# Convolution FFNs: high weights times high and low h as one 512-column matmul, sum kept in SBUF

## The chip, the cores and the metric

The kernel runs on one core of one Trainium2 chip. The metric is the device time of one execution in microseconds. A profile of one execution gives the start and duration of each instruction on TensorE (PE, with its weight loads as PEld), VectorE (DVE), ScalarE (ACT) and GpSimd (POOL), and the DMAs.

## The reference, cut to what matters

Two blocks of two layers each work on 256 positions of width 1024 in float32. Each layer of the first block ends with a feed-forward network whose up product goes through a causal depthwise convolution of three taps, before the gate:

```
h = _rmsnorm(x, norm_ffn[l]) * (1 + sc_f) + sh_f
u = _causal_dwconv(h @ ffn_w_up[l], ffn_conv_w[l], ffn_conv_b[l])   # 3 taps over time, plus a bias
ua, uv = jnp.split(u, 2, axis=-1)
x = x + g_f * ((jax.nn.silu(ua) * uv) @ ffn_w_down[l])
```

`h @ ffn_w_up` is 256 x 1024 by 1024 x 5632, the down product 256 x 2816 by 2816 x 1024. Each layer of the second block has two feed-forward networks of the same sizes without the convolution: `(silu(x @ w1) * (x @ w3)) @ w2`. So there are two convolution FFNs and four plain ones, and one piece of code, `ffn`, serves both kinds (`conv` true or false).

## The kernel before, in words

Everything is held transposed, features on the 128 partitions and the 256 positions (T) in the free dimension. An FFN is cut into 22 units (NJ = 22). Unit j takes 128 columns of the first half of the up weights (half 0, which goes through silu), 128 of the second half (half 1), and 128 rows of the down weights: 24 tiles of 128x128, one slot of 1.5 MB in a ring of four slots which SyncE fills.

A float32 product is made from three float32r products: weights and activations are split in a high and a low part, and high x high, high x low and low x high are summed. For each unit:

- ACT copies the up weights (L660, 2048 columns) and the down weights (L673, 1024 columns) to the high tile `w_hi`; DVE subtracts to get `w_lo` (L711, L716). Both tiles have two places, j % 2.
- PE's `up_pair` makes the up product of both halves. Where `conv` holds it goes by `narrow_half` (L597): for each half 8 matmuls w_hi x h_hi, 8 w_hi x h_lo, 8 w_lo x h_hi, all of 256 columns into the same 256 columns of PSUM, both halves in one bank (4 + j % 2). Plain FFNs go by `wide_half`: `hh` holds h_hi and h_lo side by side, and 8 matmuls of 512 columns (L606) give both products side by side in a bank of their own; 8 of 256 columns (L610) add w_lo x h_hi to the first 256. Only half 0 of the first unit is narrow there.
- Plain: ACT copies columns 256 to 511 to `cv` in SBUF (L685), DVE adds columns 0 to 255 to it (L742). ACT's silu (L688), DVE's product (L746).
- Convolution: ACT reads the product in PSUM, times the last tap plus the bias, into `cv` (L679, scale and bias are columns of `par`). DVE adds the other two taps, reading PSUM shifted by one and by two positions (L729, L734; two instructions each, one for each half). ACT's silu (L682), DVE's product (L746).
- Both: ACT makes `g_hi` (L693), DVE `g_lo` (L751), and PE's `down` multiplies (L634, 24 matmuls of 256 columns into banks 0 to 3, which accumulate over the 22 units).

The order is written out by hand and each engine works in order. PE: up of unit j + 1, then down of unit j. ACT for unit j: up weights of unit j + 1, down weights of j, `cv`, silu, `g_hi`. DVE for unit j: `w_lo` up of unit j + 1, `w_lo` down of j, the taps or adds, product, `g_lo`. Units 0, 1 and 18 to 21 are written out ("peeled"); units 2 to 17 run on ACT and DVE in a hardware loop of four units a turn, where the columns of `par` are addressed through registers. After unit 21 DVE adds the result to `x` (L849), which ends the stage; the next stage needs all of `x`.

Of the kernel before, what the change touches and what calls it, by code (L numbers as in the profile page):

```python
# [18 lines left out]
ALU = mybir.AluOpType  # L19
ACT = mybir.ActivationFunctionType  # L20
AX = mybir.AxisListType.X

P = 128
T = 256
# [193 lines left out]
def build(nc, A, out, layers1=LAYERS, layers2=LAYERS, dump=None):  # L218
    ctx = ExitStack()
    with ctx:  # L220
# [51 lines left out]
        def S(name):  # L272
            if name not in sems:
                sems[name] = scope[-1].enter_context(nc.semaphore(name))
            return sems[name]
# [301 lines left out]
        UP = slice(0, 2 * UNIT)  # L577
        DOWN = slice(2 * UNIT, 3 * UNIT)

        def up_out(j, half, conv):  # L580

            return bank[4 + j % 2][:, half * T:half * T + T] if conv else bank[4 + 2 * (j % 2) + half][:, :]

        def ffn_pe(pe, tag, conv):

            def narrow_half(j, half, free, first):

                for n, (w_, part) in enumerate(((w_hi, 0), (w_hi, 1), (w_lo, 0))):
                    if n == 2:
                        pe.wait_ge(*free)  # L590
                    for k in range(KD):
                        if first and n < 2:
                            pe.wait_ge(*(h_lo_ready(tag, k) if part else (S(tag + "_h_hi"), k + 1)))
                        c0 = half * UNIT + k * P
                        out = up_out(j, half, conv)
                        cols = slice(0, T) if conv or part == 0 else slice(T, 2 * T)
                        m = pe.matmul(out[:, cols], w_[:, j % 2, c0:c0 + P], hh[:, k, part, :],  # L597
                                      start=n == 0 and k == 0, stop=n == 2 and k == KD - 1, skip_group_check=True)
                return m

            def wide_half(j, half, free):

                out = up_out(j, half, conv)
                for k in range(KD):
                    c0 = half * UNIT + k * P
                    pe.matmul(out, w_hi[:, j % 2, c0:c0 + P], hh[:, k, :, :], start=k == 0, stop=False)  # L606
                pe.wait_ge(*free)
                for k in range(KD):
                    c0 = half * UNIT + k * P
                    m = pe.matmul(out[:, 0:T], w_lo[:, j % 2, c0:c0 + P], hh[:, k, 0, :], start=False,  # L610
                                  stop=k == KD - 1)
                return m

            def up_pair(j, lo_n, free_n=None, first=False):
                pe.wait_ge(S(tag + "_up_hi"), lo_n)
                if free_n is not None:
                    pe.wait_ge(S(tag + "_whole"), free_n)
                for half in range(2):
                    if first and half == 1:
                        pe.wait_ge(S(tag + "_first_hi"), 1)  # L620
                    low = (S(tag + "_first_lo"), 1) if first and half else (S(tag + "_up_lo"), lo_n)
                    if conv or (first and half == 0):
                        m = narrow_half(j, half, low, first and half == 0)
                    else:
                        m = wide_half(j, half, low)
                m.then_inc(S(tag + "_up"), 1)

            def down(j, n, first=False, last=False):
                pe.wait_ge(S(tag + "_down_lo"), n)
                pe.wait_ge(S(tag + "_g_lo"), n)  # L630
                for m_ in range(KD):
                    for p_, (w_, g_) in enumerate(((w_hi, g_hi), (w_hi, g_lo), (w_lo, g_hi))):
                        c0 = 2 * UNIT + m_ * P
                        mm = pe.matmul(acc[m_ // 2][:, m_ % 2 * T:m_ % 2 * T + T], w_[:, j % 2, c0:c0 + P],  # L634
                                       g_[:, j % 2, :],
                                       start=first and m_ % 2 == 0 and p_ == 0, stop=last and p_ == 2,
                                       skip_group_check=True)
                mm.then_inc(S(tag + "_down"), 1)

            up_pair(0, 1, first=True)  # L640
            up_pair(1, 2)
            down(0, 1, first=True)
            with pe.Fori(0, (NJ - 2) // 2) as i:
                for u in range(2):

                    up_pair(u, i * 2 + (u + 3), i * 2 + (u + 1))
                    down(u + 1, i * 2 + (u + 2))
            down(NJ - 1, NJ, last=True)
# [13 lines left out]
        def ffn_act(act, a, tag, base, conv):  # L662
            def one(j, n, w, peel=False, full_n=None):
# [10 lines left out]
                act.wait_ge(S(tag + "_up"), n)  # L674
                if late:
                    act.wait_ge(S(tag + "_g_lo"), n - 2)
                if conv:
                    for half in range(2):
                        act.activation(cv[:, j % 2, half, :], up_out(j, half, conv), ACT.Identity,  # L679
                                       scale=w(half * 4 + 2), bias=w(half * 4 + 3)).then_inc(S(tag + "_part"), 1)  # L680
                    act.wait_ge(S(tag + "_whole_a"), n)
                    act.activation(sil[:, j % 2, :], cv[:, j % 2, 0, :], ACT.Silu).then_inc(S(tag + "_silu"), 1)  # L682
                else:
                    for half in range(2):
                        act.activation(cv[:, j % 2, half, :], up_out(j, half, conv)[:, T:2 * T],  # L685
                                       ACT.Copy).then_inc(S(tag + "_part"), 1)
                    act.wait_ge(S(tag + "_whole_a"), n)
                    act.activation(sil[:, j % 2, :], cv[:, j % 2, 0, :], ACT.Silu).then_inc(S(tag + "_silu"), 1)  # L688

# [11 lines left out]
            with act.Fori(0, rounds) as i:  # L701
                for u in range(RING):
                    def w(k, u=u):
                        return par[:, bass.ds(i * (RING * 8) + (PAR1["fconv"] + (u + 2) * 8 + k), 1)]
# [14 lines left out]
        def ffn_dve(dve, tag, base, conv):  # L719
            def one(j, n, w, peel=False, more=True):  # L720
                if more:
                    split_up_low(dve, tag, base, j + 1, n + 1)
                split_down_low(dve, tag, base, j, n)
                if conv:

                    dve.wait_ge(S(tag + "_part"), n * 2)
                    for half in range(2):
                        dst, src = cv[:, j % 2, half, :], up_out(j, half, conv)
                        dve.scalar_tensor_tensor(dst[:, 1:T], src[:, 0:T - 1], w(half * 4 + 1), dst[:, 1:T], ALU.mult,  # L729
                                                 ALU.add).then_inc(S(tag + "_tap1"), 1)  # L730
                    dve.wait_ge(S(tag + "_tap1"), n * 2)
                    for half in range(2):
                        dst, src = cv[:, j % 2, half, :], up_out(j, half, conv)
                        dve.scalar_tensor_tensor(dst[:, 2:T], src[:, 0:T - 2], w(half * 4), dst[:, 2:T], ALU.mult,  # L734
                                                 ALU.add).then_inc(S(tag + ("_whole" if half else "_whole_a")), 1)
                    dve.wait_ge(S(tag + "_whole"), n)
                else:

                    dve.wait_ge(S(tag + "_part"), n * 2)
                    for half in range(2):  # L740
                        dst = cv[:, j % 2, half, :]
                        dve.tensor_tensor(dst, up_out(j, half, conv)[:, 0:T], dst,  # L742
                                          ALU.add).then_inc(S(tag + ("_whole" if half else "_whole_a")), 1)
                    dve.wait_ge(S(tag + "_whole"), n)
                dve.wait_ge(S(tag + "_silu"), n)
                dve.tensor_tensor(sil[:, j % 2, :], sil[:, j % 2, :], cv[:, j % 2, 1, :], ALU.mult).then_inc(S(tag + "_g"), 1)  # L746

                dve.wait_ge(S(tag + "_g_hi"), n)
                if not peel:
                    dve.wait_ge(S(tag + "_down"), n - 2)  # L750
                dve.tensor_tensor(g_lo[:, j % 2, :], sil[:, j % 2, :], g_hi[:, j % 2, :],  # L751
                                  ALU.subtract).then_inc(S(tag + "_g_lo"), 1)
# [13 lines left out]
        def ffn(tag, stream, layer, base, conv, weight, shift, finish, loaded, more, params=None):  # L766


            nonlocal w_hi, w_lo, hh, g_hi, g_lo, sil, cv
            phase = ExitStack()  # L770
            phases["n"] += 1

# [4 lines left out]
            hh = buf("hh", [P, KD, 2, T], F32R)  # L777
            g_hi, g_lo = buf("g_hi", [P, 2, T], F32R), buf("g_lo", [P, 2, T], F32R)
            sil, cv = buf("sil", [P, 2, T]), buf("cv", [P, 2, 2, T])
            with phase, nc.Block() as block:  # L780
                @block.sync
                def _(sp):
# [67 lines left out]
                                                 x[:, j, :], ALU.mult, ALU.add).then_inc(S(tag + "_x"), 1)  # L850
                    dve.wait_ge(S(tag + "_x"), KD)

        w_hi = w_lo = hh = g_hi = g_lo = sil = cv = None

        def pcol_(name, j, table):
            return par[:, table[name] + j:table[name] + j + 1]
# [1242 lines left out]
```

## Time and profile before

| | |
|---|---|
| three runs | 2810.98, 2815.16, 2817.90 us; median 2815.16 |
| the profiled execution | 2814.93 us, its span 2812.9 us |
| busy share of the span | PE 90%, PEld 74%, DVE 51%, ACT 37%, POOL 7% |
| instructions | 37494 |
| DMA | 391.28 MB, mean 139 GB/s |

The two convolution FFNs lie at about 669 to 872 us and 1345 to 1548 us of the span. A row of the timeline gives the start, the time from the first start to the last end, the engine, the line, output and inputs, and how many instructions are merged in it; in brackets the idle time of the engine before it and what ended it. Neighbours on one engine overlap a little, so that the distance of two starts is shorter than a duration.

### The profile page before, as it was taken

How to read it: one execution, taken by the hardware profiler on the slowest of the kernel's cores; microseconds unless marked ns; L12 is line 12 of the kernel's file. 1: busy time of each engine (PE TensorE's matmuls, PEld its weight loads, DVE VectorE, ACT ScalarE, POOL GpSimd, SP SyncE). 2: the span in 40 equal slices, each digit the busy share in tenths (PEclk: the TensorE clock that was granted, in tenths of full speed). 3: DMA queues.
4: the chain of work that ended last, by engine and by line, in shares of the span. 5: the costliest groups of instructions: out<-in, count | busy, mean ns of one | idle time of the engine just before them, and what ended most of it. 6: DMA issues, size and time to landing. Idle time of an engine off the chain costs nothing. (4 is left out here: it accounts for less than half of the span.)

```text
span 2812.9 us, 37494 instructions
## 1 busy us (share of the span) xinstructions
PE 2533.0 (90%) x13806; PEld 2077.3 (74%) x13806; DVE 1440.3 (51%) x2574; ACT 1028.0 (37%) x1847; POOL 198.2 (7%) x225
## 2 busy tenths in 40 slices
PE   8998999998997999989899799867998799867997
PEld 2236677777996767778899699645997699646996
DVE  7803562424673456141676565374654555374554
ACT  1003334213553333321554444222544454222553
POOL 0000000011000000001100100431000100431000
PEclk9999999998998999999899899978999899978998
DMA  8754332233543322323442545212451554202550
GB/s 303 259 186 184 113 113 90 90 121 134 194 157 118 115 110 91 113 83 141 158 179 90 203 179 201 86 42 90 179 181 43 211 194 180 105 23 90 190 190 38
DMA packets 37258, 391.28 MB, mean 139 GB/s; under 512 B 4384, under 2 KB 5024, under 8 KB 5408
## 3 DMA queue, kind: packets, MB, share of 16 engines
q1 hardware_dynamic: 37152, 389.92, 37.9%
q8 instruction: 60, 0.98, 0.1%
q14 instruction: 46, 0.38, 0.0%
HBM read 388.85 MB, written 1.05 MB: 139 GB/s over the span
## 5 line engine op out<-in xcount | busy, mean ns | idle before, releaser
L1088 PE MATMUL bank<-h,ring 128*128 128x256 f32 x2048 | 475.4, 389 | 33.3 <-ACT h L997 28.3
L1088 PEld LDWEIGHTS bank<-h,ring 128*128 128x128 f32 x2048 | 394.2, 194 | 111.1 <-issue 37.9
L711 DVE TENSOR_TENSOR ffn_w_lo<-ring,ffn_w_hi 128x2048 fp32r<-128x2048 f32 x126 | 288.9, 2293 | 167.6 <-ACT ffn_w_hi L660 167.6
L606 PE MATMUL bank<-ffn_hh,ffn_w_hi 128*128 128x512 f32 x1376 | 347.6, 395 | 0.0
L634 PE MATMUL bank<-ffn_g_hi,ffn_w_hi 128*128 128x256 f32 x1056 | 299.3, 283 | 4.5 <-DVE ffn_g_lo L751 4.5
L634 PE MATMUL bank<-ffn_g_lo,ffn_w_hi 128*128 128x256 f32 x1056 | 298.8, 283 | 0.0
L634 PE MATMUL bank<-ffn_g_hi,ffn_w_lo 128*128 128x256 f32 x1056 | 298.8, 283 | 0.0
L597 PE MATMUL bank<-ffn_hh,ffn_w_hi 128*128 128x256 f32 x1472 | 217.0, 299 | 81.5 <-ACT ffn_hh L810 81.2
L606 PEld LDWEIGHTS bank<-ffn_hh,ffn_w_hi 128*128 128x128 f32 x1376 | 250.1, 191 | 45.0
L597 PEld LDWEIGHTS bank<-ffn_hh,ffn_w_hi 128*128 128x128 f32 x1472 | 197.6, 201 | 93.9 <-issue 77.4
L660 ACT ACTIVATE ffn_w_hi<-ring 128x2048 fp32r<-128x2048 f32 x126 | 239.9, 1904 | 0.0
L634 PEld LDWEIGHTS bank<-ffn_g_hi,ffn_w_hi 128*128 128x128 f32 x1056 | 202.7, 192 | 5.6 <-issue 5.6
L634 PEld LDWEIGHTS bank<-ffn_g_hi,ffn_w_lo 128*128 128x128 f32 x1056 | 202.7, 192 | 0.0
L634 PEld LDWEIGHTS bank<-ffn_g_lo,ffn_w_hi 128*128 128x128 f32 x1056 | 202.7, 192 | 0.0
L1088 PE MATMUL bank<-work,ring 128*128 128x256 f32 (+1 forms) x880 | 201.4, 384 | 0.4 <-DVE work L1447 0.4
L610 PEld LDWEIGHTS bank<-ffn_hh,ffn_w_lo 128*128 128x128 f32 x1376 | 187.7, 190 | 13.4
L1088 PEld LDWEIGHTS bank<-work,ring 128*128 128x128 f32 (+1 forms) x880 | 166.1, 190 | 36.4 <-issue 8.5
L610 PE MATMUL bank<-ffn_hh,ffn_w_lo 128*128 128x256 f32 x1376 | 191.9, 282 | 0.0
L398 PE MATMUL bank<-ring,cact 128*1 128x512 f32 x384 | 168.4, 598 | 2.5 <-DMA ring<-ada_in 1.7
L1230 ACT ACTIVATE work<-bank 128x256 f32<-128x256 f32 (+2 forms) x168 | 63.9, 381 | 285.2 <-PE bank L1088 280.5
L716 DVE TENSOR_TENSOR ffn_w_lo<-ring,ffn_w_hi 128x1024 fp32r<-128x1024 f32 x132 | 160.9, 1219 | 4.9 <-ACT ffn_w_hi L673 4.9
L557 DVE SCALAR_TENSOR_TENSOR work<-bank,work 128x512 f32<-128x512 f32 (+2 forms) x52 | 31.6, 608 | 243.4 <-ACT work L934 141.0
(251 smaller groups left out, 3213.0 us busy)
## 6 DMA issues: line engine op xcount, KB each, us to landing
ring<-s_in SPq DMA_DIRECT2D x212, 1536.0 KB, 6.4
ring<-ada_in SPq DMA_DIRECT2D x32, 1536.0 KB, 6.8
work<-mem_in SPq DMA_DIRECT2D x2, 1024.0 KB, 4.9
x<-x_in SPq DMA_DIRECT2D x1, 1024.0 KB, 6.3
y_out<-x SPq DMA_DIRECT2D x1, 1024.0 KB, 3.9
con<-con_in SPq DMA_DIRECT2D x1, 801.0 KB, 4.7
par<-par_in SPq DMA_DIRECT2D x2, 302.0 KB, 3.7
work<-pos_in SPq DMA_DIRECT2D x2, 128.0 KB, 3.6
```

Of the source, the lines that this page charges most:

```text
L398: m = pe.matmul(bank[1 + 2 * (g_ % 2) + half][0:1, :], cact[:, k:k + 1], ring[:, slot % RING, c0:c0 + 4 * P], start=k == 0, stop=k == KD - 1)
L557: dve.scalar_tensor_tensor(spare, ps, width * EPS, rs, ALU.add, ALU.mult).then_inc(read, 1)
L597: m = pe.matmul(out[:, cols], w_[:, j % 2, c0:c0 + P], hh[:, k, part, :], start=n == 0 and k == 0, stop=n == 2 and k == KD - 1, skip_group ...
L606: pe.matmul(out, w_hi[:, j % 2, c0:c0 + P], hh[:, k, :, :], start=k == 0, stop=False)
L610: m = pe.matmul(out[:, 0:T], w_lo[:, j % 2, c0:c0 + P], hh[:, k, 0, :], start=False, stop=k == KD - 1)
L634: mm = pe.matmul(acc[m_ // 2][:, m_ % 2 * T:m_ % 2 * T + T], w_[:, j % 2, c0:c0 + P], g_[:, j % 2, :], start=first and m_ % 2 == 0 and p_ ...
L660: act.activation(w_hi[:, j % 2, UP], ring[:, slot, UP], ACT.Copy).then_inc(S(tag + "_up_hi"), 1)
L711: dve.tensor_tensor(w_lo[:, j % 2, UP], ring[:, (base + j) % RING, UP], w_hi[:, j % 2, UP], ALU.subtract).then_inc(S(tag + "_up_lo"), 1)
L716: dve.tensor_tensor(w_lo[:, j % 2, DOWN], ring[:, (base + j) % RING, DOWN], w_hi[:, j % 2, DOWN], ALU.subtract).then_inc(S(tag + "_down_lo ...
L1088: m = pe.matmul(ps[0:m_rows, 0:T], tile(t0 + k)[:, 0:m_rows], rhs, start=k == 0, stop=k == len(src) - 1 and kind != "uk")
L1230: act.activation(dst[0:m_rows, :], bank[i % 2][0:m_rows, 0:T], ACT.Copy).then_inc(S("pj_free"), 1)
```

## The change

`up_out` gives the convolution FFNs the banks of the plain ones, and `up_pair` sends them through `wide_half` (only half 0 of unit 0 stays narrow, with its high x low product in the second 256 columns). ACT and DVE first make the sum in `cv`, as in the plain FFN (one copy and one add for each half). Then ACT makes tap 0 from `cv` into a new tile `tp`, DVE adds taps 1 and 2, reading `cv`, and silu and product read `tp`. PE's wait for a free bank is for the two adds of unit n - 2 in place of the taps.

```diff
-                    if conv or (first and half == 0):
+                    if first and half == 0:
                         m = narrow_half(j, half, low, first and half == 0)
                     else:
                         m = wide_half(j, half, low)
...
+                for half in range(2):
+                    act.activation(cv[:, j % 2, half, :], up_out(j, half)[:, T:2 * T],
+                                   ACT.Copy).then_inc(S(tag + "_part"), 1)
                 if conv:
                     for half in range(2):
-                        act.activation(cv[:, j % 2, half, :], up_out(j, half, conv), ACT.Identity,
-                                       scale=w(half * 4 + 2), bias=w(half * 4 + 3)).then_inc(S(tag + "_part"), 1)
-                    act.wait_ge(S(tag + "_whole_a"), n)
-                    act.activation(sil[:, j % 2, :], cv[:, j % 2, 0, :], ACT.Silu).then_inc(S(tag + "_silu"), 1)
+                        act.wait_ge(S(tag + "_whole"), 2 * n + (half - 1))
+                        act.activation(tp[:, j % 2, half, :], cv[:, j % 2, half, :], ACT.Identity,
+                                       scale=w(half * 4 + 2), bias=w(half * 4 + 3)).then_inc(S(tag + "_tap0"), 1)
+                    act.wait_ge(S(tag + "_tap2_a"), n)
+                    act.activation(sil[:, j % 2, :], tp[:, j % 2, 0, :], ACT.Silu).then_inc(S(tag + "_silu"), 1)
...
+                for half in range(2):
+                    dve.wait_ge(S(tag + "_part"), n * 2 + (half - 1))
+                    dst = cv[:, j % 2, half, :]
+                    dve.tensor_tensor(dst, up_out(j, half)[:, 0:T], dst,
+                                      ALU.add).then_inc(S(tag + ("_whole" if half or conv else "_whole_a")), 1)
                 if conv:
-
-                    dve.wait_ge(S(tag + "_part"), n * 2)
                     for half in range(2):
-                        dst, src = cv[:, j % 2, half, :], up_out(j, half, conv)
+                        dve.wait_ge(S(tag + "_tap0"), n * 2 + (half - 1))
+                        dst, src = tp[:, j % 2, half, :], cv[:, j % 2, half, :]
                         dve.scalar_tensor_tensor(dst[:, 1:T], src[:, 0:T - 1], w(half * 4 + 1), dst[:, 1:T], ALU.mult,
                                                  ALU.add).then_inc(S(tag + "_tap1"), 1)
-                    dve.wait_ge(S(tag + "_tap1"), n * 2)
                     for half in range(2):
-                        dst, src = cv[:, j % 2, half, :], up_out(j, half, conv)
+                        dve.wait_ge(S(tag + "_tap1"), n * 2 + (half - 1))
+                        dst, src = tp[:, j % 2, half, :], cv[:, j % 2, half, :]
                         dve.scalar_tensor_tensor(dst[:, 2:T], src[:, 0:T - 2], w(half * 4), dst[:, 2:T], ALU.mult,
-                                                 ALU.add).then_inc(S(tag + ("_whole" if half else "_whole_a")), 1)
-                    dve.wait_ge(S(tag + "_whole"), n)
+                                                 ALU.add).then_inc(S(tag + ("_tap2" if half else "_tap2_a")), 1)
+                    dve.wait_ge(S(tag + "_tap2"), n)
```

## Rows read from the trace of the kernel before

**Rows 1.** Windows: stretch; length, busy us and counts by engine, PEclk, DMA share, GB/s

```profile
350.00:400.00 50.00, 47.66 (x214) 37.81 (x213) 32.40 (x85) 14.70 (x46) 0.00 (x0) 0.93 0.26 95
...
750.00:800.00 50.00, 50.00 (x419) 50.00 (x419) 34.22 (x48) 27.20 (x35) 0.00 (x0) 1.00 0.52 189
```

**Rows 2.** Timeline of PE: up of two convolution units, then of two plain units

```profile
700.03 2.08 PE L597 MATMUL bank<-ffn_hh,ffn_w_hi 128*128 128x256 f32 x16
...
708.67 2.08 PE L597 MATMUL bank<-ffn_hh,ffn_w_hi 128*128 128x256 f32 x16
...
2052.43 2.00 PE L606 MATMUL bank<-ffn_hh,ffn_w_hi 128*128 128x512 f32 x8
...
2060.90 1.32 PE L606 MATMUL bank<-ffn_hh,ffn_w_hi 128*128 128x512 f32 x5
```

**Rows 3.** Timeline of DVE, first convolution FFN, units 2 and 3

```profile
700.02 0.87 DVE L729 SCALAR_TENSOR_TENSOR ffn_cv<-bank,par,ffn_cv 128x255 f32<-128x255 f32 x2
701.03 0.87 DVE L734 SCALAR_TENSOR_TENSOR ffn_cv<-bank,par,ffn_cv 128x254 f32<-128x254 f32 x2
702.07 0.42 DVE L746 TENSOR_TENSOR ffn_sil<-ffn_sil,ffn_cv 128x256 f32<-128x256 f32 x1 [0.16 <-ACT ffn_sil L682]
...
706.99 1.22 DVE L716 TENSOR_TENSOR ffn_w_lo<-ring,ffn_w_hi 128x1024 fp32r<-128x1024 f32 x1
708.13 0.86 DVE L729 SCALAR_TENSOR_TENSOR ffn_cv<-bank,par,ffn_cv 128x255 f32<-128x255 f32 x2
```

**Rows 4.** Timeline of ACT and DVE, unit 17 (in the loop), then unit 18 (peeled)

```profile
827.10 1.02 ACT L679 ACTIVATE ffn_cv<-bank,par 128x256 f32<-128x256 f32 x2 [1.79 <-PE bank L597]
828.26 0.87 DVE L729 SCALAR_TENSOR_TENSOR ffn_cv<-bank,par,ffn_cv 128x255 f32<-128x255 f32 x2 [0.44 <-ACT ffn_cv L679]
...
835.60 1.02 ACT L679 ACTIVATE ffn_cv<-bank,par 128x256 f32<-128x256 f32 x2 [1.65 <-PE bank L597]
836.65 0.87 DVE L729 SCALAR_TENSOR_TENSOR ffn_cv<-bank,par,ffn_cv 128x255 f32<-128x255 f32 x2 [0.19 <-ACT ffn_cv L679]
```

**Rows 5.** Timeline of ACT and DVE in a plain FFN: add and silu

```profile
2058.91 0.76 DVE L742 TENSOR_TENSOR ffn_cv<-bank,ffn_cv 128x256 f32<-128x256 f32 x2 [1.25 <-ACT ffn_cv L685]
2059.37 0.42 ACT L688 ACTIVATE ffn_sil<-ffn_cv 128x256 f32<-128x256 f32 x1 [0.49 <-DVE ffn_cv L742]
```

**Rows 6.** Groups by line and shape: count, busy us, mean ns of one, idle before

```profile
L685 ACT ACTIVATE ffn_cv<-bank 128x256 f32<-128x256 f32 x176 | 57.9, 381 | 266.9 <-PE bank L610 266.9
L679 ACT ACTIVATE ffn_cv<-bank,par 128x256 f32<-128x256 f32 x88 | 44.9, 561 | 76.8 <-PE bank L597 76.8
L729 DVE SCALAR_TENSOR_TENSOR ffn_cv<-bank,par,ffn_cv 128x255 f32<-128x255 f32 x88 | 38.4, 478 | 26.9 <-ACT ffn_cv L679 26.9
L567 DVE SCALAR_TENSOR_TENSOR h<-x,acol,rs_x 128x256 f32<-128x256 f32 x32 | 13.0, 481 | 0.1
```

**Rows 7.** Timeline, start of the first convolution FFN: unit 0 on ACT and DVE

```profile
682.96 1.02 ACT L679 ACTIVATE ffn_cv<-bank,par 128x256 f32<-128x256 f32 x2 [4.88 <-PE bank L597]
683.99 1.28 ACT L682 ACT_TABLE_LOAD   x1
685.96 0.42 DVE L746 TENSOR_TENSOR ffn_sil<-ffn_sil,ffn_cv 128x256 f32<-128x256 f32 x1 [0.17 <-ACT ffn_sil L682]
```

**Rows 8.** Timeline of DVE, end of that FFN: units 20 and 21, then x

```profile
855.87 0.43 DVE L746 TENSOR_TENSOR ffn_sil<-ffn_sil,ffn_cv 128x256 f32<-128x256 f32 x1 [0.16 <-ACT ffn_sil L682]
857.74 1.23 DVE L716 TENSOR_TENSOR ffn_w_lo<-ring,ffn_w_hi 128x1024 fp32r<-128x1024 f32 x1 [0.52 <-ACT ffn_w_hi L673]
864.51 0.42 DVE L746 TENSOR_TENSOR ffn_sil<-ffn_sil,ffn_cv 128x256 f32<-128x256 f32 x1 [0.17 <-ACT ffn_sil L682]
869.14 3.23 DVE L849 SCALAR_TENSOR_TENSOR x<-bank,mod,x 128x256 f32<-128x256 f32 x8 [3.29 <-PE bank L634]
```

**Rows 9.** The same two marks of DVE in the second convolution FFN

```profile
1361.70 0.42 DVE L746 TENSOR_TENSOR ffn_sil<-ffn_sil,ffn_cv 128x256 f32<-128x256 f32 x1 [0.17 <-ACT ffn_sil L682]
...
1544.88 3.23 DVE L849 SCALAR_TENSOR_TENSOR x<-bank,mod,x 128x256 f32<-128x256 f32 x8 [3.28 <-PE bank L634]
```

More of the change, by code:

```diff
@@ L578, in build, with up_out @@
         DOWN = slice(2 * UNIT, 3 * UNIT)
-        def up_out(j, half, conv):
-            return bank[4 + j % 2][:, half * T:half * T + T] if conv else bank[4 + 2 * (j % 2) + half][:, :]
+        def up_out(j, half):
+            return bank[4 + 2 * (j % 2) + half][:, :]
         def ffn_pe(pe, tag, conv):
@@ L594, in narrow_half @@
                         c0 = half * UNIT + k * P
-                        out = up_out(j, half, conv)
-                        cols = slice(0, T) if conv or part == 0 else slice(T, 2 * T)
+                        out = up_out(j, half)
+                        cols = slice(part * T, part * T + T)
                         m = pe.matmul(out[:, cols], w_[:, j % 2, c0:c0 + P], hh[:, k, part, :],
@@ L601, in wide_half @@
             def wide_half(j, half, free):
-                out = up_out(j, half, conv)
+                out = up_out(j, half)
                 for k in range(KD):
@@ L616, in up_pair @@
                 if free_n is not None:
-                    pe.wait_ge(S(tag + "_whole"), free_n)
+                    pe.wait_ge(S(tag + "_whole"), 2 * free_n if conv else free_n)
                 for half in range(2):
@@ L676, in one @@
                     act.wait_ge(S(tag + "_g_lo"), n - 2)
+                for half in range(2):
+                    act.activation(cv[:, j % 2, half, :], up_out(j, half)[:, T:2 * T],
+                                   ACT.Copy).then_inc(S(tag + "_part"), 1)
                 if conv:
                     for half in range(2):
-                        act.activation(cv[:, j % 2, half, :], up_out(j, half, conv), ACT.Identity,
-                                       scale=w(half * 4 + 2), bias=w(half * 4 + 3)).then_inc(S(tag + "_part"), 1)
-                    act.wait_ge(S(tag + "_whole_a"), n)
-                    act.activation(sil[:, j % 2, :], cv[:, j % 2, 0, :], ACT.Silu).then_inc(S(tag + "_silu"), 1)
-                else:
-                    for half in range(2):
-                        act.activation(cv[:, j % 2, half, :], up_out(j, half, conv)[:, T:2 * T],
-                                       ACT.Copy).then_inc(S(tag + "_part"), 1)
+                        act.wait_ge(S(tag + "_whole"), 2 * n + (half - 1))
[3 more added lines that the diff above has]
+                    act.activation(sil[:, j % 2, :], tp[:, j % 2, 0, :], ACT.Silu).then_inc(S(tag + "_silu"), 1)
+                else:
                     act.wait_ge(S(tag + "_whole_a"), n)
@@ L734, in one @@
                         dve.scalar_tensor_tensor(dst[:, 2:T], src[:, 0:T - 2], w(half * 4), dst[:, 2:T], ALU.mult,
-                                                 ALU.add).then_inc(S(tag + ("_whole" if half else "_whole_a")), 1)
-                    dve.wait_ge(S(tag + "_whole"), n)
-                else:
[L739 to L743, printed above, removed]
+                                                 ALU.add).then_inc(S(tag + ("_tap2" if half else "_tap2_a")), 1)
@@ L744, in one @@
+                    dve.wait_ge(S(tag + "_tap2"), n)
+                else:
                     dve.wait_ge(S(tag + "_whole"), n)
                 dve.wait_ge(S(tag + "_silu"), n)
-                dve.tensor_tensor(sil[:, j % 2, :], sil[:, j % 2, :], cv[:, j % 2, 1, :], ALU.mult).then_inc(S(tag + "_g"), 1)
+                other = (tp if conv else cv)[:, j % 2, 1, :]
+                dve.tensor_tensor(sil[:, j % 2, :], sil[:, j % 2, :], other, ALU.mult).then_inc(S(tag + "_g"), 1)
                 dve.wait_ge(S(tag + "_g_hi"), n)
@@ L766, in ffn @@
         def ffn(tag, stream, layer, base, conv, weight, shift, finish, loaded, more, params=None):
-            nonlocal w_hi, w_lo, hh, g_hi, g_lo, sil, cv
+            nonlocal w_hi, w_lo, hh, g_hi, g_lo, sil, cv, tp
             phase = ExitStack()
@@ L779, in ffn @@
             sil, cv = buf("sil", [P, 2, T]), buf("cv", [P, 2, 2, T])
+            if conv:
+                tp = buf("tp", [P, 2, 2, T])
             with phase, nc.Block() as block:
@@ L851, in _ @@
                     dve.wait_ge(S(tag + "_x"), KD)
-        w_hi = w_lo = hh = g_hi = g_lo = sil = cv = None
+        w_hi = w_lo = hh = g_hi = g_lo = sil = cv = tp = None
         def pcol_(name, j, table):
```

## The prediction

> **What bounds the kernel now.** I read the windows first. In the middle of a convolution FFN PE is busy for all 50.00 us at the full clock, in 419 matmuls of 256 columns [rows 1]. The timeline of PE gives one unit: 708.67 - 700.03 = 8.64 us for 72 matmuls, 0.120 each. A plain FFN's unit starts 8.47 us after the last (2052.43 to 2060.90) with 56 matmuls, 16 of them of 512 columns [rows 2]. So PE sets the pace, and the wide form is worth 8.64 - 8.47 = 0.17 us a unit.
>
> The second question is how far behind PE the others are, and the first units answer it. There DVE comes late out of the norm and never waits for the product; units run at the pace of a loop that goes through ACT and DVE. From tap 1 of unit 2 to that of unit 3 it is 708.13 - 700.02 = 8.11 us, with no wait ahead of the taps [rows 3]. The loop is: taps, silu, product, g_hi, then, since ACT works in order, the high copy of the next up weights, on DVE their low part, the low part of the down weights, and the taps again. Later PE is the slower one (8.64) and DVE idles 0.44 us ahead of the taps [rows 4]. The margin of that loop under PE is thus 8.64 - 8.11 = 0.53 us now, and after the change PE's own pace is 8.47, a margin of 0.36.
>
> **PE's part of the change.** 43 of 44 halves in each of two stages go wide: about 21.5 x 0.17 = 3.7 us a stage, 7.3 in all, if PE stays the bound. Its wait for a free bank is met by the adds of two units back, earlier than by the taps: nothing. For the 0.17 the trace has both forms [rows 2]. The Trainium skill (TensorE: Matmul & The Clock Gate, Back-to-back issue gap) gives 262 cycles for 256 columns and 518 for 512, which would make it 16 x 2.5 ns = 0.04 us; the rows show four times that, and it matters only if PE is the bound.
>
> **The loop's part.** Two copies of PSUM on ACT take the place of the two scaled ones and end before DVE gets there, as now in the early units. What is new stands in a row: add (DVE), tap 0 (ACT, from SBUF), tap 1 (DVE). I count from the start of the first add to the start of the first tap 2, in a unit of the hardware loop:
> - add to tap 0: a plain FFN's silu starts 2059.37 - 2058.91 = 0.46 after the add that it waits for [rows 5]. An instruction whose `par` columns are addressed through registers starts later after its wait: DVE's tap 1 starts 0.14 after the pair on ACT ended in unit 17 (828.26 - 828.12) and 0.03 in unit 18, which is peeled (836.65 - 836.62); ACT's pair came 8.50 after the one before when peeled, against 8.64 [rows 4]. So 0.14 more: tap 0 of half 0 at 0.60, half 1 at 1.02 - 0.56 = 0.46 later [rows 4, 6], at 1.06.
> - tap 0 itself isn't in the trace. From PSUM with two pointers it takes 0.561, the copy without pointers 0.381 [rows 6], so the pointers cost 0.18; from SBUF without them ACT takes 0.42 [rows 5]. I take 0.60 (bounds 0.42 and 0.60). Half 0 ends at 1.20, half 1 at 1.66.
> - tap 1 of half 0 at 1.20 + 0.14 = 1.34, of half 1 at 1.66 + 0.14 = 1.80; tap 2 follows one spacing later (0.87 - 0.478 = 0.39 [rows 3, 6]), its own wait and addresses being hidden behind tap 1: 2.19.
>
> From tap 2 round to the next add nothing changes: 708.13 - 701.03 = 7.10 us [rows 3]. The new loop is 7.10 + 2.19 = 9.29 us, 0.82 over PE's 8.47. PE no longer bounds these stages; it waits in `down` for g_lo. In peeled units without the register time: tap 0 at 0.46 and 0.92, tap 1 at 1.09 and 1.55, tap 2 at 1.94, loop 9.04. Per-half waits are in this; what the former double wait cost (1.01 between taps 1 and 2) goes.
>
> DVE's taps read SBUF in place of PSUM. 478 ns from PSUM, 481 from SBUF for the same operation [rows 6]: nothing. The Trainium skill (VectorE: DVE Perf Modes, Rules for kernel authors) advises to copy a matmul's output to SBUF first if many operations follow, and its section on the TRN2 errata gives 62 cycles less of fixed cost from SBUF, 65 ns. If each tap were shorter by that, one or two of them per round would count, 0.07 to 0.13 us, and the sum would be 3 to 5 us lower; the rows show no such difference.
>
> **Sum for one stage**, from DVE's product of unit 0 to the first update of x. Before: 869.14 - 685.96 = 183.18 [rows 7, 8], and the same 183.18 in the second stage [rows 9].
> - Start: before, silu's table was loaded (1.28) while DVE did the taps [rows 7]. Now ACT has the tap 0s ahead of it: copies from about 682.86, add at 683.27, tap 0 of half 1 ends 683.27 + 0.92 + 0.60 = 684.79, table until 686.08, product at 686.62: +0.66.
> - Product of unit 0 to that of unit 20: 16 units of the hardware loop x 9.29, 4 peeled x 9.04, and 0.3 for three turns of ACT's loop (an estimate, a tenth each): 185.1. Before 855.87 - 685.96 = 169.91 [rows 7, 8]. +15.2.
> - End: unit 21 has no further up weights, so the loop is short. Low part of down 1.87 after the product of unit 20 (857.74 - 855.87), add 1.14 later (708.13 - 706.99 [rows 3]), tap 2 1.94 later, product 1.04 later (702.07 - 701.03): 5.99, then 869.14 - 864.51 = 4.63 to x: 10.62. Before 869.14 - 855.87 = 13.27 [rows 8], where it waited for PE. -2.65.
>
> Together +13.2 a stage, +26.4 in all. The profiled execution took 2814.93 us, 2.0 more than its span and 0.2 under the median of 2815.16; forecast 2841.5 against the median, of which I take 2840, since more bounds lie below than above.
>
> The extra DVE work (two adds, 0.76 a unit) and ACT's (two instructions) are in these terms. Ring slots come free up to 0.8 us a unit later, but PE, DVE and ACT ask for them later too, and DMA moves half of what it could (share 0.52 [rows 1]). PE has slack of its own: the products of unit n + 1 are ready some 2.7 us before the loop wants them, so PE's waits don't add up with the loop's.
>
> **Rivals.**
> - The insertion is cheap: no register time, tap 0 at 0.42. Tap 1 at 0.91 and 1.37, tap 2 at 1.76, loop 8.86 everywhere, 20 x 8.86 + 0.3 = 177.5, +7.6 + 0.5 - 2.8 = +5.3 a stage: 2826; with the register time for some, 2832. For it: sequencers may fetch addresses while the engine works. Against: rows 4.
> - Dearer: register time also ahead of tap 0 of half 1 and of tap 2, +0.21 a loop unit, 6.7 in all: 2848.
> - The clock: PE with waits of 0.8 in 9.3 us. In a mixer's stretch with PE busy 47.66 of 50 the granted clock was 0.93 [rows 1], some 7 us at the 1.2 GHz level, in which PE gives up 3.5 us; 2.7 are covered by PE's slack. Four such spells a stage would add up to 3 us, 6 in all: 2847.
> - PE stays the bound: 2815.2 - 7.3 + about 1 for a longer last chain = 2809. It needs the insertion to fit in the 0.36 us margin; add, tap 0 and their hand-overs are 1.18 by the cheapest rows. It decides for faster from a loop of 8.47 down; for no change the loop must be near 8.65.
> - The wide products don't come about (more waits in PE's stream): PE would be at 8.64, still under 9.29, so the time would be the same as forecast.
>
> **Chances.** Forecast (loop 9.15 to 9.45, 2836 to 2846) 0.55; cheap 0.22; dearer or clock 0.15; no change 0.04; PE stays the bound 0.04. Range 2826 to 2849. About 0.3%, 8 us, is what a measurement can tell from no change. Faster 0.03, same 0.04, slower 0.93.
>
> **What would show it.** After: DVE's adds with no wait for ACT's copies, ACT's tap 0 near 0.60 us, product to product 9.3 us in units 2 to 17 and 9.0 in the peeled ones; PE in groups of 8 matmuls of 512 columns, with an idle time of about 0.8 us ahead of `down`, released by g_lo, in each unit; DVE busy 76% of a unit; both stages longer by 13 us and nothing else changed. I am wrong if PE still shows 50.00 of 50 in the windows, or if the distance of two products is under 8.7 us.

## The result, and the profile after

The changed kernel took 2839.99 us (2837.47 to 2842.98, four runs), the kernel before 2813.07 (2810.15 to 2817.90, four runs): ratio 1.0094, 95% interval 1.0076 to 1.0113. It is slower by 27 us. Its profiled execution took 2842.98 us, with a span of 2841.2.

First the windows of the changed kernel, two of convolution FFNs and one of a plain one (columns as in [rows 1]):

```profile
750.00:800.00 50.00, 46.08 (x302) 41.69 (x302) 34.82 (x53) 29.17 (x43) 0.00 (x0) 1.00 0.48 176
...
1400.00:1450.00 50.00, 46.10 (x297) 41.42 (x295) 35.83 (x56) 27.80 (x44) 0.00 (x0) 1.00 0.50 177
...
2050.00:2100.00 50.00, 50.00 (x333) 46.02 (x332) 29.50 (x37) 25.59 (x36) 0.00 (x0) 1.00 0.51 189
```

PE, busy for all 50 us before, is now busy for 46, at the same full clock, and only in the convolution FFNs. Its timeline there shows where the idle time lies:

```profile
782.44 2.00 PE L606 MATMUL bank<-ffn_hh,ffn_w_hi 128*128 128x512 f32 x8
784.28 1.11 PE L610 MATMUL bank<-ffn_hh,ffn_w_lo 128*128 128x256 f32 x8
785.23 2.00 PE L606 MATMUL bank<-ffn_hh,ffn_w_hi 128*128 128x512 f32 x8
787.08 1.11 PE L610 MATMUL bank<-ffn_hh,ffn_w_lo 128*128 128x256 f32 x8
788.83 0.36 PE L634 MATMUL bank<-ffn_g_hi,ffn_w_hi 128*128 128x256 f32 x1 [0.64 <-DVE ffn_g_lo L751]
791.77 2.00 PE L606 MATMUL bank<-ffn_hh,ffn_w_hi 128*128 128x512 f32 x8
```

The up products are the wide ones, and from one up to the next it is 791.77 - 782.44 = 9.33 us, against 8.64 before [rows 2]. PE waits ahead of `down`, for g_lo. From 700 to 860 us of the span the waits by engine say the same of 17 units (total, times, longest):

```profile
PE bank L634 <- DVE ffn_g_lo L751: 11.2, 17, 0.9
```

DVE and ACT in one unit of the hardware loop, which answers to [rows 3, 5] (in two views, DVE first):

```profile
764.03 1.22 DVE L717 TENSOR_TENSOR ffn_w_lo<-ring,ffn_w_hi 128x1024 fp32r<-128x1024 f32 x1
765.16 0.75 DVE L728 TENSOR_TENSOR ffn_cv<-bank,ffn_cv 128x256 f32<-128x256 f32 x2
766.51 0.97 DVE L734 SCALAR_TENSOR_TENSOR ffn_tp<-ffn_cv,par,ffn_tp 128x255 f32<-128x255 f32 x2 [0.60 <-ACT ffn_tp L683]
767.41 0.87 DVE L739 SCALAR_TENSOR_TENSOR ffn_tp<-ffn_cv,par,ffn_tp 128x254 f32<-128x254 f32 x2
768.44 0.43 DVE L746 TENSOR_TENSOR ffn_sil<-ffn_sil,ffn_tp 128x256 f32<-128x256 f32 x1 [0.16 <-ACT ffn_sil L686]
769.35 0.43 DVE L751 TENSOR_TENSOR ffn_g_lo<-ffn_sil,ffn_g_hi 128x256 fp32r<-128x256 f32 x1 [0.48 <-ACT ffn_g_hi L694]
771.26 2.29 DVE L712 TENSOR_TENSOR ffn_w_lo<-ring,ffn_w_hi 128x2048 fp32r<-128x2048 f32 x1 [1.49 <-ACT ffn_w_hi L660]
```

```profile
761.69 1.04 ACT L673 ACTIVATE ffn_w_hi<-ring 128x1024 fp32r<-128x1024 f32 x1
762.63 0.64 ACT L678 ACTIVATE ffn_cv<-bank 128x256 f32<-128x256 f32 x2
765.77 1.09 ACT L683 ACTIVATE ffn_tp<-ffn_cv,par 128x256 f32<-128x256 f32 x2 [2.50 <-DVE ffn_cv L728]
767.91 0.42 ACT L686 ACTIVATE ffn_sil<-ffn_tp 128x256 f32<-128x256 f32 x1 [1.05 <-DVE ffn_tp L739]
768.90 0.42 ACT L694 ACTIVATE ffn_g_hi<-ffn_sil 128x256 fp32r<-128x256 f32 x1 [0.56 <-DVE ffn_sil L746]
769.31 1.92 ACT L660 ACTIVATE ffn_w_hi<-ring 128x2048 fp32r<-128x2048 f32 x1
```

Neither engine waits for PE any more: ACT reads PSUM (762.63) with no wait ahead of it and then idles 2.50 us for DVE's add. Each waits only for the other, all the way round. DVE is busy 6.5 of 9.33 us and ACT 5.4 (34.82 and 29.17 of 50 in the first window above). Nobody is full, and still nobody can go faster.

A measure that leaves the rest of the program out is the stage: from ACT's first instruction for the norm (L551) to the first update of x. Before it was 869.14 - 663.04 = 206.10 and 206.19 us, after 882.89 - 660.89 = 222.00 and 221.97. The two stages grew by 31.7; the span grew by 28.3, since the rest of the program came out 3.4 us shorter in this execution. Such differences in parts that no edit touched came in all the runs, with some us to either side, so below I give the stages of a kernel beside its ratio.

### The profile page after: what moved, and what is told of

Its sections match the earlier page's. It is cut to its first block and busy times, and to the rows that moved or that the text cites. A ratio compares the mean times of both kernels' runs of the same rounds, so it can differ in the third digit from the quotient of the medians.

```text
span 2841.2 us, 36330 instructions
## 1 busy us (share of the span) xinstructions
PE 2530.0 (89%) x13118; PEld 2040.4 (72%) x13118; DVE 1470.4 (52%) x2662; ACT 1054.5 (37%) x1935; POOL 196.5 (7%) x225
## 5 line engine op out<-in xcount | busy, mean ns | idle before, releaser
L606 PE MATMUL bank<-ffn_hh,ffn_w_hi 128*128 128x512 f32 x2064 | 521.5, 395 | 0.0
L606 PEld LDWEIGHTS bank<-ffn_hh,ffn_w_hi 128*128 128x128 f32 x2064 | 375.2, 191 | 67.5
L610 PEld LDWEIGHTS bank<-ffn_hh,ffn_w_lo 128*128 128x128 f32 x2064 | 281.6, 190 | 20.1
L610 PE MATMUL bank<-ffn_hh,ffn_w_lo 128*128 128x256 f32 x2064 | 287.6, 282 | 0.0
L678 ACT ACTIVATE ffn_cv<-bank 128x256 f32<-128x256 f32 x264 | 86.0, 377 | 295.8 <-PE bank L610 295.8
L728 DVE TENSOR_TENSOR ffn_cv<-bank,ffn_cv 128x256 f32<-128x256 f32 x264 | 99.4, 418 | 124.9 <-ACT ffn_cv L678 124.9
```

The source lines that it names most:

```text
L678: act.activation(cv[:, j % 2, half, :], up_out(j, half)[:, T:2 * T], ACT.Copy).then_inc(S(tag + "_part"), 1)
L728: dve.tensor_tensor(dst, up_out(j, half)[:, 0:T], dst, ALU.add).then_inc(S(tag + ("_whole" if half or conv else "_whole_a")), 1)
```

## The experiments

The loop theory: ACT and DVE in turn set the pace. Rivals: the wide products cost; the engines' busy time is the limit; the gain of anything that helps is its own and has nothing to do with the loop.

**Narrow products, new chain.**

```diff
-                    if first and half == 0:
+                    if conv or (first and half == 0):
                         m = narrow_half(j, half, low, first and half == 0)
```

> The changed kernel, but PE's up products of the convolution FFNs in the narrow form (72 matmuls of 256 columns a unit, the high x low product in the second 256 columns), with the new chain on ACT and DVE. Loop theory: the ACT-DVE loop of 9.33 us a unit sets the pace and PE's 8.64 is under it, so the time stays that of the changed kernel, 2838 to 2842 us, with PE's idle time before down falling from about 0.65 to about 0.5 us a unit or less. Rival (the 512-column products or their banks are what costs): back to 2813 to 2820.

Ratio to before 1.0136 (1.0119 to 1.0153), median 2846.33 us; stages 222.04 and 220.94. Its windows and two of its units on DVE:

```profile
750.00:800.00 50.00, 47.14 (x384) 46.09 (x383) 34.82 (x54) 28.73 (x43) 0.00 (x0) 1.00 0.49 182
```

```profile
756.68 0.75 DVE L728 TENSOR_TENSOR ffn_cv<-bank,ffn_cv 128x256 f32<-128x256 f32 x2
...
766.01 0.75 DVE L728 TENSOR_TENSOR ffn_cv<-bank,ffn_cv 128x256 f32<-128x256 f32 x2
```

9.33 us a unit, with 72 matmuls in place of 56: PE's form makes no difference to the pace, as the loop theory has it, and the rival falls. PE's waits ahead of `down` shrank, as its own work grew by 0.17 us: 0.71 and 0.46 us in two units where the changed kernel has 0.89 and 0.64. The median lies 4 us above what I expected, and the interval lies above that of the changed kernel (1.0076 to 1.0113). Where those us went stays open: the profiled execution, 2840.36 us, was the fastest of the four, the other three took 2846 to 2848 us, and their stages aren't seen. The second stage is 1.1 us shorter than the first because TensorE's clock fell in the last `down` of the first one alone (more on that below).

**Wide products, no taps.** The three taps are left out; silu and the product read the sum.

```diff
 # ACT
-                        act.activation(tp[:, j % 2, half, :], cv[:, j % 2, half, :], ACT.Identity, ...
-                    act.activation(sil[:, j % 2, :], tp[:, j % 2, 0, :], ACT.Silu)...
+                    act.wait_ge(S(tag + "_whole"), 2 * n - 1)
+                    act.activation(sil[:, j % 2, :], cv[:, j % 2, 0, :], ACT.Silu)...
 # DVE: taps 1 and 2 out
```

> The changed kernel with tap 0, 1 and 2 left out of the convolution FFNs (silu and product read the sum); the wide products stay. Loop theory: the loop loses 2.2 us and PE bounds both stages at 8.47 a unit, 7.3 us under the kernel before: 2804 to 2808 us, PE 50.00 of 50 busy. Rival (wide products cost): at or over 2813.

Ratio 0.9966 (0.9955 to 0.9977), 2798.87 us; stages 200.75 and 201.09, PE 50.00 of 50 busy, 8.47 us a unit. The stages are 5.2 us shorter each: the wide form was forecast to give 3.7 (measured by itself further down, 3.4), and PE's wait ahead of the last `down` went from 1.64 to 0.04 us, which I hadn't counted. The median is some 5 us under my range; 3 of these are in the stages, and the kernel before ran at 2810.45 beside this one, not at 2813.

**Tap 0 left out.** ACT's copy goes, DVE's first tap writes `tp` from the unshifted sum.

```diff
-                        act.activation(tp[:, j % 2, half, :], cv[:, j % 2, half, :], ACT.Identity, ...
...
-                        dve.wait_ge(S(tag + "_tap0"), n * 2 + (half - 1))
-                        dve.scalar_tensor_tensor(dst[:, 1:T], src[:, 0:T - 1], w(half * 4 + 1), dst[:, 1:T], ...
+                        dve.wait_ge(S(tag + "_whole"), n * 2 + (half - 1))
+                        dve.scalar_tensor_tensor(dst[:, 0:T], src[:, 0:T], w(half * 4 + 1), src[:, 0:T], ...
```

> The changed kernel with tap 0 and the bias left out: ACT makes no scaled copy, DVE's first tap reads the unshifted sum twice and writes tp itself. Theory (the way from DVE to ACT and back is on the loop: from the first add to tap 1 1.34 us in place of the 0.7 of two adds): the loop falls by some 0.6 to 0.75 us a unit, to 8.6 to 8.7, 20 units of it 12 to 15 us a stage, stages near 208 us: 2812 to 2818 us. Rival (DVE's busy time, which this leaves as it is at 6.98 us a unit, sets the pace): 9.33 stays, 2838 to 2842.

Ratio 1.0008 (0.9996 to 1.0020), 2811.27 us; stages 205.87 and 205.96. DVE:

```profile
750.64 0.75 DVE L724 TENSOR_TENSOR ffn_cv<-bank,ffn_cv 128x256 f32<-128x256 f32 x2
751.31 0.87 DVE L730 SCALAR_TENSOR_TENSOR ffn_tp<-ffn_cv,par 128x256 f32<-128x256 f32 x2
752.10 0.87 DVE L735 SCALAR_TENSOR_TENSOR ffn_tp<-ffn_cv,par,ffn_tp 128x254 f32<-128x254 f32 x2
...
759.19 0.75 DVE L724 TENSOR_TENSOR ffn_cv<-bank,ffn_cv 128x256 f32<-128x256 f32 x2
```

The loop is 759.19 - 750.64 = 8.55 us, from the first unit of the stage on. DVE has as much to do as in the changed kernel (37.66 of 50 us busy, 6.4 us a unit in place of 6.5), so busy time isn't the limit. Add to tap 1 is 0.67 here and 1.35 with the way to ACT and back; tap 1 to tap 2 is 0.79 and 0.90. Together that is 9.33 - 8.55 = 0.78 us a unit, and the stages are back at the 206 us of the kernel before. In the written-out units the difference is 0.52 (9.07 against 8.55): that is the price of the hop itself, one ACTIVATE of 0.6 us and two hand-overs. The other 0.26 is what the next experiment takes away. PE's row in the windows reads 50.00 of 50 here although its own pace is 8.47: 0.08 us a unit is too little to show, since the modelled end of a matmul lies 0.16 after the start of the next. The stages hold 1.5 us of low clock each, in the last `down`.

**Fixed parameter columns in the loop.** Units 2 to 17 use the columns of units 2 to 5.

```diff
-                        return par[:, bass.ds(i * (RING * 8) + (PAR1["fconv"] + (u + 2) * 8 + k), 1)]
+                        return par[:, PAR1["fconv"] + (u + 2) * 8 + k:PAR1["fconv"] + (u + 2) * 8 + k + 1]
```

> The changed kernel, but in ACT's and DVE's loop of four units the parameter columns are fixed (those of units 2 to 5 serve all units of the loop), so that no register is added to in front of tap 0, 1 and 2. Theory (address work behind a wait costs 0.26 us a unit, 9.33 against 9.07 in the written-out units): units 2 to 17 come at 9.07, 16 x 0.26 = 4.2 us a stage less, 8 in all: about 2832 us. Rival (the written-out units are faster for another reason, such as no loop): 9.33 stays, 2838 to 2842.

Ratio 1.0095 (1.0079 to 1.0110), 2835.66 us; stages 217.29 and 218.28, 4.7 and 3.7 shorter. From unit 0 to unit 20 both are 4.8 shorter; in the second stage the whole last `down` ran at the low clock, which cost 1.1 us more than in the first. About 2832 us had been expected.

```profile
744.60 1.22 DVE L717 TENSOR_TENSOR ffn_w_lo<-ring,ffn_w_hi 128x1024 fp32r<-128x1024 f32 x1
745.74 0.75 DVE L728 TENSOR_TENSOR ffn_cv<-bank,ffn_cv 128x256 f32<-128x256 f32 x2
746.82 0.97 DVE L734 SCALAR_TENSOR_TENSOR ffn_tp<-ffn_cv,par,ffn_tp 128x255 f32<-128x255 f32 x2 [0.34 <-ACT ffn_tp L683]
```

Add to tap 1 is 1.08 in place of 1.35, and the units of the loop come at 9.07, like the written-out ones. Addresses made from registers behind a wait do cost 0.26 us a unit: they start tap 0 0.16 later (add to tap 0 0.61 in the loop, 0.45 written out) and tap 1 0.10 later (from tap 0's start 0.74 and 0.64). Against before this kernel looks no better than the changed one by its ratio; its stages say that it is.

**The high copy of the up weights made early.** The loop has a way round: ACT idles 2.5 us ahead of tap 0, and its 1.9 us copy, for which DVE waits 1.3 to 1.5 us, needs only that PE is through with unit j.

```diff
-                if full_n is not None:
+                if full_n is not None and not conv:
                     split_up_high(act, tag, base, j + 1, full_n, None if peel and j == 0 else n - 1)
...
                 if conv:          # behind the copies from PSUM
+                    if far_n is not None:
+                        split_up_high(act, tag, base, j + 2, far_n, None)
                     for half in range(2):
                         act.wait_ge(S(tag + "_whole"), 2 * n + (half - 1))
...
+            if conv:
+                split_up_high(act, tag, base, 1, occ(1), None)
```

> The changed kernel, with ACT's high copy of the up weights made one unit ahead: in unit j that of unit j + 2, between the copies from PSUM and tap 0, where ACT idled 2.5 us. It then no longer stands between g_hi and DVE's low part, where DVE waited 1.3 us. Loop theory: the loop falls to about 8.05 us, under PE's 8.47; PE bounds again: 2806 to 2812 us. Rival (DVE's and ACT's work as such, or the wide products, set the time): about 2840 or a few us under. Second rival: tap 0 queued behind the early copy lengthens the chain, and half of the gain is kept: 2820 to 2830.

Ratio 1.0003 (0.9989 to 1.0017), 2811.10 us; stages 205.79 and 205.84. All 27 us are gone. PE is the bound again:

```profile
750.00:800.00 50.00, 50.00 (x332) 45.99 (x331) 39.72 (x60) 30.56 (x48) 0.00 (x0) 1.00 0.50 187
```

But the 3.7 us a stage of the wide form didn't show. PE's timeline has what took it (first down of the stage, then the last):

```profile
687.77 0.36 PE L634 MATMUL bank<-ffn_g_hi,ffn_w_hi 128*128 128x256 f32 x1 [1.20 <-DVE ffn_g_lo L756]
...
862.28 0.36 PE L634 MATMUL bank<-ffn_g_hi,ffn_w_hi 128*128 128x256 f32 x1 [2.07 <-DVE ffn_g_lo L756]
862.47 0.28 PE L634 MATMUL bank<-ffn_g_lo,ffn_w_hi 128*128 128x256 f32 x1
...
863.58 0.42 PE L634 MATMUL bank<-ffn_g_hi,ffn_w_hi 128*128 128x256 f32 x1
863.80 0.41 PE L634 MATMUL bank<-ffn_g_lo,ffn_w_hi 128*128 128x256 f32 x1
```

In unit 0 tap 0 stood behind the early copy, and PE waited 1.20 us; the last wait grew from 1.64 to 2.07; and in the last `down` the matmuls go over to nearly twice their spacing (0.21 in place of 0.12; granted clock 0.57 from 863 to 867 us), the 1.2 GHz level, which costs 1.5 us: from the last product to x it is 6.12 us in place of 4.62. The three make 3.1 us.

**The same edit in the kernel before.**

> The kernel before, with the same early high copy in its convolution FFNs. Loop theory: PE bounds it at 8.64 a unit already, so nothing is to be had: 2811 to 2815 us. Rival (the early copy is a gain by itself, for instance at the start of a stage): 2805 or less.

Ratio 1.0008 (0.9996 to 1.0020), 2810.78 us; stages 206.74 twice, 0.6 longer than before. Where PE is the bound the early copy has nothing to give.

**The start mended.** In unit 0 the early copy goes behind g_hi, and silu's table is loaded before the wait for the product.

```diff
+                if conv and peel and j == 0:
+                    act.preload_act_table_set("silu_and_others")
                 act.wait_ge(S(tag + "_up"), n)
...
-                    if far_n is not None:
+                    if far_n is not None and not (peel and j == 0):
                         split_up_high(act, tag, base, j + 2, far_n, None)
...
                 act.activation(g_hi[:, j % 2, :], sil[:, j % 2, :], ACT.Copy).then_inc(S(tag + "_g_hi"), 1)
+                if conv and peel and j == 0:
+                    split_up_high(act, tag, base, 2, far_n, None)
```

> The early high copy on top of the changed kernel, with the start mended: in unit 0 the early copy comes after g_hi, and silu's table is loaded before the wait for the up product. Theory (the first experiment of this kind gave back 1.2 us at down of unit 0, 0.4 of wait and 1.3 of low clock at the end of each stage): PE's wait of 1.20 us at down of unit 0 goes, 1.2 us a stage, 2.4 in all under it: about 2808 us, 0.1% under the kernel before. Rival (the start is not on the path): as that one, 2811.

Ratio 0.9972 (0.9961 to 0.9983), 2803.33 us; stages 203.05 and 203.04. This beats both kernels: 3.1 us a stage under the one before, 19 a stage under the changed one. PE goes through the first `down` without a wait, 1.2 us as expected; the rest of the difference to the kernel without the mended start, 1.5 us a stage, is that the clock did not fall at the end. That I had not expected (about 2808 us), and no edit was aimed at it. With the early copy the loop itself takes 7.94 us (units 1 to 4; I had expected about 8.05), under PE's 8.47. The silu table in ACT's timeline now lies in ACT's idle time:

```profile
678.08 1.28 ACT L675 ACT_TABLE_LOAD   x1
682.91 0.66 ACT L680 ACTIVATE ffn_cv<-bank 128x256 f32<-128x256 f32 x2 [3.55 <-PE bank L610]
683.78 1.10 ACT L687 ACTIVATE ffn_tp<-ffn_cv,par 128x256 f32<-128x256 f32 x2 [0.22 <-DVE ffn_cv L737]
```

**The same with narrow products** (the edit of the first experiment).

> The mended early-copy kernel, with PE's up products of the convolution FFNs in the narrow form. Theory (with the loop out of PE's way the whole gain over the kernel before is the wide form's 0.17 us a unit): units at 8.64 again, a stage of 206 to 207 us against 203.05 wide and 206.15 before: 2809 to 2812 us, no change against the kernel before. Rival (the gain is that of the early copy or of the mended start): about 2803, like the wide one.

Ratio 0.9996 (0.9987 to 1.0006), 2810.46 us; stages 206.45 and 206.44, 8.64 a unit. So the wide form is worth 206.44 - 203.05 = 3.4 us a stage, once the loop is below PE's pace, and the gain over the kernel before is that: with narrow products the same kernel is level with it.

**The last wait filled.** PE makes matmuls of 512 columns, which nobody reads, in its last wait: nine on top of the mended kernel, twelve on top of the changed one.

```diff
+            if conv:
+                pe.wait_ge(S(tag + "_whole"), 2 * NJ - 2)
+                for k in range(9):
+                    pe.matmul(bank[4][:, :], w_hi[:, 1, 0:P], hh[:, k % KD, :, :], start=True, stop=True)
             down(NJ - 1, NJ, last=True)
```

> As the mended one, and PE fills its last wait (2.07 us between down of unit 20 and down of unit 21) with nine matmuls of 512 columns whose result nobody reads. Theory (the idle time ahead of the last down lets the clock fall and doubles half of that down): the clock stays at full, and 1.3 us a stage, 2.6 in all, go: about 2805 us. Rival (the clock falls for another reason): no gain or 0.2 us more a stage.

Ratio 0.9973 (0.9962 to 0.9984), 2804.04 us; stages 203.32 and 203.05. No gain: in the mended kernel the clock hadn't fallen, with the same 2.07 us of wait as where it had, so this run doesn't test the theory.

> The changed kernel, with twelve matmuls of 512 columns, unread, in PE's last wait of 2.91 us. Theory: full clock in the last down, from its first matmul to x 3.1 us in place of 4.4, 1.3 us a stage, 2.6 in all: about 2837 us. Rival (the clock falls for another reason): 2840 as before, with the low clock still seen.

Ratio 1.0085 (1.0070 to 1.0100), 2833.56 us; stages 220.72 and 220.69, 1.3 us shorter each, as expected, with full clock in both last downs. By the ratios (1.0094 to 1.0085, with intervals that overlap) the kernel fell by about 2.5 us; these are 2.6. The medians differ by more, 6.4 us, but the kernel before, too, ran 2.2 us faster beside this one (2810.85 against 2813.07).

## Why the prediction was right, point by point

The forecast was 2840 us, the measured time 2839.99. That close a hit has luck in it: the stages grew by 31.7 us where I had 26.4, and the rest of the program gave 3.4 back. My sum was 2841.5, and I took 2840 because more bounds lay below than above; the terms that were off lay above. The sum also starts from 2815.16, while the kernel before had a median of 2813.07 beside the changed one.

- PE bounds before, the ACT-DVE loop at 8.11 is just behind: right. It was to be read from the first units of the stage, where the loop ran alone; the busy shares (DVE 51%) said nothing of it. The reason that I gave, DVE late out of the norm, was wrong: in unit 0 ACT waits 4.88 us for the product [rows 7] and DVE then 3.35 for ACT. They fall behind in unit 1, because PE makes the up products of units 0 and 1 in a row, 5.76 us apart (their last matmuls end at 682.91 and 688.67), and the loop needs 8.00.
- The loop: 9.29 predicted, 9.33 measured; 9.04 and 9.07 in the written-out units. Its pieces: add to tap 0 0.60 and 0.61, tap 0 0.60 and 0.595, add to tap 1 1.34 and 1.35, add to tap 2 2.19 and 2.25. Tap 0's price, made from the pointers' cost in PSUM (0.561 - 0.381 [rows 6]) and the copy from SBUF (0.42 [rows 5]), held. The register work, which I had at 0.14 ahead of tap 0 and again ahead of tap 1, is 0.16 and 0.10; the fixed columns showed that it is the registers.
- Taps reading SBUF in place of PSUM: 477 ns for tap 2 against 478. Tap 1 took 484. By the table of the Trainium skill (VectorE: DVE Perf Modes, the TRN2 errata) it would have been 65 ns less; the runs don't show it.
- Start: +0.66 predicted. From L551 to the first product 684.48 - 660.89 = 23.59, before 685.96 - 663.04 = 22.92: +0.67.
- Units 0 to 20: +15.2 predicted, 870.99 - 684.48 = 186.51 against 169.91: +16.6 measured. The turns of the loop cost 0.16 each, not 0.1; each unit 0.04 more than I had; and unit 19 was 0.37 us late in both stages, with DVE waiting 0.52 between silu and product where it is 0.16 in units 1 to 18, 20 and 21. It came in all kernels with taps by the new chain and with the loop's registers, at that unit, and not with fixed columns. I did not find its cause.
- End: -2.65 predicted, 11.90 against 13.27 measured, -1.4. The step that was mis-sized is the last down: I took 4.63 from product to x, it was 882.89 - 877.00 = 5.89. The clock rival had named the mechanism and put it in the wrong place, on the units with slack, where the granted clock stayed at 1.00. It fell after PE's last and longest wait (granted clock 0.68 from 878 to 883 us), and the spacing went from 0.12 to 0.21:

```profile
878.48 0.35 PE L634 MATMUL bank<-ffn_g_hi,ffn_w_hi 128*128 128x256 f32 x1 [2.91 <-DVE ffn_g_lo L751]
...
879.62 0.28 PE L634 MATMUL bank<-ffn_g_hi,ffn_w_hi 128*128 128x256 f32 x1
879.74 0.34 PE L634 MATMUL bank<-ffn_g_lo,ffn_w_hi 128*128 128x256 f32 x1
879.88 0.41 PE L634 MATMUL bank<-ffn_g_hi,ffn_w_lo 128*128 128x256 f32 x1
880.09 0.42 PE L634 MATMUL bank<-ffn_g_hi,ffn_w_hi 128*128 128x256 f32 x1
```

  Filling that wait gave the 1.3 us back.
- PE's wait ahead of `down`: 0.8 predicted, 0.66 on average (11.2 over 17). The pace of PE alone, 8.47, and the loop's 9.33 differ by 0.86; the row counts from the modelled end of the last matmul, which is 0.16 after the next one could have started, and behind the wait the first matmul is followed after 0.19 in place of 0.12.
- DVE busy 76% of a unit predicted: 34.82 of 50 us, 70%. I had added up durations, and neighbours overlap. Nothing in the sum hung on it.
- The worth of the wide form if PE is the bound: 3.7 us a stage predicted, 3.4 measured. The cycle counts of the Trainium skill (TensorE: Matmul & The Clock Gate, Back-to-back issue gap) would have made it 0.04 a unit, an estimate from that page; the runs have 0.17.

## What to carry to other kernels

Before an engine that sets the pace is relieved, look for the loop right behind it: the start of a stage, where the late engine catches up, shows its pace with no other limit. Here 0.53 us of margin were there, the edit put 1.2 us into that loop to save 0.17 on PE, and gave the gain only after work that had no need to be in the loop (a copy that could be made a unit ahead) was taken out. An operation that is handed to another engine and back lengthens such a loop however idle both engines are by their busy shares: here 0.52 us a unit for an operation of 0.6 us, and 0.26 more where its columns were addressed through registers.

## What the runs showed of the hardware that I had not expected

- TensorE's clock after a wait isn't told by the wait alone. After a last wait of 1.64 us (two kernels) it stayed up. After 2.07 us it fell to the 1.2 GHz level within the next `down` in both stages of one kernel and in neither stage of two others; after 2.37 us (tap 0 left out) in both stages; after 2.90 us in both stages of two kernels and in one of two in a third. It did not fall where the wait was filled. What decides between two equal waits stays open.
- An operand whose column is addressed through registers makes its instruction start later behind a wait, 0.10 us on DVE (tap 1) and 0.16 on ACT (tap 0), and no later where instructions are queued already: tap 1 to tap 2 is 0.90 us in the loop and in the written-out units.
